# Two-layer trunk with an expert mixture: one product of two columns per item, smaller products in two levels, other order at entry and end

## The chip, the cores and the metric

One core of a Trainium2 chip runs the whole program. The metric is the device time of the program in microseconds, the median of repeated executions. The profile page and the trace come from one further execution.

## The reference

256 frames of width 1024 pass two layers, in fp32. Layer 0 is a gated mixer, a SwiGLU of width 2816 and a gated embedding; the change does not touch it. Layer 1 is a gated linear recurrence (HGRN2) with 8 heads of 128, the expert SwiGLU with 2 of 8 experts per frame, and again the gated embedding:

```python
def hgrn2(h, w_in, lb, o_norm_g, w_out):
    ...
    attn = jnp.einsum('bhtk,bhsk,bhtsk->bhts', qc, kc, decay)
    o = o_inter + jnp.einsum('bhts,bhsv->bhtv', attn, ic)
    ...
    o = rms_norm(o, o_norm_g.reshape(C_HEADS, C_HEAD_DIM)).reshape(bsz, s, C_WIDTH)
    return (o * jax.nn.silu(g)) @ w_out

def moe_swiglu(h, w_router, b_router, w_gu, w_down):
    logits = (h @ w_router) + b_router
    top_logit, top_idx = lax.top_k(logits, TOP_K)
    gates = ...
    for e in range(N_EXPERTS):
        out = out + gates[..., e:e + 1] * swiglu(h, w_gu[e], w_down[e])
    return out

gate = jax.nn.sigmoid(x @ ple_w_gate[layer])
x = x + gate * (p[layer] @ ple_w_proj[layer])
```

## The kernel before

**Products in three parts.** Every large weight is cut into granules of 128x2048 fp32, loaded by SP's DMAs. ScalarE rounds a granule to its high part (`hi`, L968, two instructions of 128x1024), VectorE subtracts to get the low part (`lo`, L1330, two instructions). A product is three matmuls of 512 columns, high by high, high by low and low by high (`split_matmul`, L451 to L453). The parts stand in a ring of 6 slots (`w_hi`, `w_lo`); the semaphores `hi_done`, `lo_done` and `used` keep the three engines in step.

**Items.** After the router, the frames of each expert are put in a list of up to 128, an item. Here 8 items run, 7 in the loop and the last behind it. An item has 7 units (`EU`) of 512 hidden columns: a unit's gate and up sides are four granules, 48 matmuls (`unit_gu`: side 0 and side 1), ScalarE takes the silu of side 0 (`unit_silu`, L1226), VectorE multiplies it by side 1 (`unit_hidden`, L1844), TensorE transposes the result (`unit_turn`, L863, 4 matmuls), ScalarE and VectorE evict it in two parts (`hT`: L1080, L1548), and the down product is two granules, 24 matmuls (`unit_down`). TensorE's order is: transposes of this unit, sides of the next one, down product of this unit, transposes of the next.

**What runs once per item.** VectorE selects the item's columns (`select`, L1784 and L1785) and compares them with a count (`compare`, L1789), which gives the one-hot matrix `sel` (frames by slots). TensorE gets from it, in the item's first unit, the frame that each slot is filled from (`turn_src`, L821, two matmuls of one column), and behind the last unit's transposes the row that each slot's result is written to (`turn_rows`: L835 adds a constant by the identity, L837 two matmuls of one column). VectorE turns both into integers (`origin`, L1868; `dst`). GpSimd gathers and stores rows by them. TensorE also transposes the gathered rows (`turn_xg`, L829).

**The entry.** The sides of the first unit are computed while the lists are made. ScalarE then waits for that product, then for the table's head (`table_ready`), and enters its loop. VectorE does `lo(77)`, `lo(78)`, select and compare, and then the first hidden product.

**The end.** Behind the last item VectorE evicts the transposed p (`pT(2)`, L1571), sums gates by rank and adds what was stored for each frame (`add_rows`, L1850 to L1858). TensorE does the last down product (`last_down`), puts the results back to frames by the transposed one-hot matrix (L944, L945; evictions L1285 and L1906), adds the projection of p (`proj_half`, 24 matmuls) and transposes the layer's output (`turn_x`, L502) for the gate.

**The recurrence's levels.** Within a block of 128 frames the decayed product of q and k is built in levels of doubling width. Before level n VectorE scales half of q and half of k (L1656, L1657); TensorE multiplies all heads (`level`, L702, 16 matmuls of 128x64); VectorE merges the result into the attention matrix under a mask (`meet`, L1634, 1.3 us). Between levels stand 12 matmuls of the input product. Behind them come the output's norm by head, a multiply of the silu gate by the norm's gain (`gains_of`, L1670) and the gate product (L1685).

## Time and profile before

| | |
|---|---|
| median of 3 executions | 1506.45 us (1506.19 to 1507.27) |
| profiled execution: its own time, its span | 1507.38 us, 1505.6 us |
| TensorE matmul busy | 98% of the span |
| TensorE weight load, VectorE, ScalarE busy | 81%, 83%, 66% |
| matmuls of the recurrence's levels 1 to 7 (L702) | 27.3 us |
| one item in the loop | 119.83 us |

### The profile page before, as it was taken

The page shows a single profiled execution, that of the slowest core. Times are in us where ns is not written, and L with a number is a line of the kernel's source. Part 1 is how long each engine was busy: PE and PEld are TensorE (multiplying, and loading weights), DVE is VectorE, ACT ScalarE, POOL GpSimd, SP SyncE. Part 2 cuts the span into 40 slices and gives each one's busy share as a digit, 9 for nine tenths or more (in the row PEclk, how much of TensorE's full clock was granted, in tenths as well). Part 3 has the DMA queues.
Part 4 walks back from the last instruction along what each step waited for, and adds up shares of the span by engine and source line. Part 5 has one row for each costly group of instructions (what it writes and reads, how often), then busy time and mean ns, then how long its engine had stood idle before and what let it go on. Part 6 is the DMA issues. An engine that isn't in the chain of part 4 may idle for free.

```text
span 1505.6 us, 23650 instructions
## 1 busy us (share of the span) xinstructions
PE 1474.3 (98%) x6913; PEld 1226.5 (81%) x6915; DVE 1244.1 (83%) x1544; ACT 1000.6 (66%) x1231; POOL 42.1 (3%) x43
## 2 busy tenths in 40 slices
PE   8999999999999899999999999999999999999988
PEld 6877888788887688888888888888888888888876
DVE  7996545574887989899988998899989889889985
ACT  6555444375225577787877877777787777778762
POOL 1000000000000200000000000000000000000000
PEclk9999999999999899999999999999999999999999
DMA  7666555555234899999999999999999999999960
GB/s 285 207 222 217 196 194 173 175 169 195 84 114 144 327 398 374 353 379 405 340 374 410 345 368 410 369 346 410 390 320 411 403 323 400 396 349 384 409 240 29
DMA packets 124743, 453.09 MB, mean 301 GB/s; under 512 B 13968, under 2 KB 13968, under 8 KB 124704
## 3 DMA queue, kind: packets, MB, share of 16 engines
q1 hardware_dynamic: 119952, 435.25, 77.3%
q0 software_dynamic: 4752, 17.34, 3.2%
q8 instruction: 22, 0.36, 0.1%
q14 instruction: 17, 0.14, 0.0%
HBM read 444.14 MB, written 8.39 MB: 301 GB/s over the span
## 4 chain that ended last, share of the span: by engine, by line
PE 92%; DVE 5%; ACT 1%; DMA 1%; issue 1%; SPq 0%; DVEq 0%; ACTq 0%
PE PS L451 29%; PE PS L453 28%; PE PS L452 28%; DVE w_lo L1330 2%; PE PS L863 2%; PE PS L702 2%; DMA raw<-in_w_in_ab 1%; PE PS L502 1%; PE PS L829 0%; ACT w_hi L968 0%; PE PS L588 0%; PE PS L809 0%; PE PS L697 0%; PE PS L746 0%; PE PS L685 0%
## 5 line engine op out<-in xcount | busy, mean ns | idle before, releaser
L1330 DVE TENSOR_TENSOR w_lo<-raw,w_hi 128x1024 fp32r<-128x1024 f32 x486 | 568.7, 1221 | 33.0 <-ACT w_hi L968 30.5
L451 PE MATMUL PS<-w_hi,xT_hi 128*128 128x512 f32 x1424 | 566.1, 398 | 5.1 <-DVE w_lo L1330 2.8
L453 PE MATMUL PS<-w_lo,xT_hi 128*128 128x512 f32 x1424 | 557.4, 391 | 0.0
L452 PE MATMUL PS<-w_hi,xT_lo 128*128 128x512 f32 x1424 | 556.3, 391 | 0.0
L968 ACT ACTIVATE w_hi<-raw 128x1024 fp32r<-128x1024 f32 x486 | 489.7, 1060 | 71.7 <-PE PS L453 44.6
L1330 DVE TENSOR_TENSOR w_lo<-SC,w_hi 128x1024 fp32r<-128x1024 f32 x340 | 392.0, 1220 | 10.9 <-ACT w_hi L968 9.3
L968 ACT ACTIVATE w_hi<-SC 128x1024 fp32r<-128x1024 f32 x340 | 337.5, 1060 | 15.3 <-PE PS L453 10.8
L451 PEld LDWEIGHTS PS<-w_hi,xT_hi 128*128 128x128 f32 x1424 | 269.8, 189 | 60.1 <-issue 5.3
L453 PEld LDWEIGHTS PS<-w_lo,xT_hi 128*128 128x128 f32 x1424 | 268.5, 189 | 57.6
L452 PEld LDWEIGHTS PS<-w_hi,xT_lo 128*128 128x128 f32 x1424 | 269.0, 189 | 53.5
L451 PE MATMUL PS<-w_hi,hT_hi 128*128 128x512 f32 x536 | 208.8, 390 | 4.2 <-DVE hT_lo L1548 4.2
L453 PE MATMUL PS<-w_lo,hT_hi 128*128 128x512 f32 x536 | 208.9, 390 | 0.0
L452 PE MATMUL PS<-w_hi,hT_lo 128*128 128x512 f32 x536 | 208.5, 389 | 0.0
L451 PEld LDWEIGHTS PS<-w_hi,hT_hi 128*128 128x128 f32 x536 | 100.6, 188 | 25.8 <-DVE hT_lo L1548 3.2
L453 PEld LDWEIGHTS PS<-w_lo,hT_hi 128*128 128x128 f32 x536 | 100.6, 188 | 20.9
L452 PEld LDWEIGHTS PS<-w_hi,hT_lo 128*128 128x128 f32 x536 | 100.6, 188 | 20.8
L1080 ACT ACTIVATE hT_hi<-PS 128x512 fp32r<-128x512 f32 x67 | 40.4, 603 | 98.0 <-PE PS L863 64.7
L1226 ACT ACTIVATE junk<-PS 128x512 f32<-128x512 f32 x56 | 33.5, 598 | 91.1 <-PE PS L453 91.0
L1548 DVE TENSOR_TENSOR hT_lo<-PS,hT_hi 128x512 fp32r<-128x512 f32 x67 | 46.3, 691 | 56.4 <-ACT hT_hi L1080 56.4
L1844 DVE TENSOR_TENSOR junk<-junk,PS 128x512 f32<-128x512 f32 x56 | 38.4, 686 | 32.5 <-ACT junk L1226 32.4
L863 PEld LDWEIGHTS PS<-ident,junk 128*128 128x128 f32 x224 | 35.4, 201 | 10.7 <-DVE junk L1844 6.5
L1542 DVE SCALAR_TENSOR_TENSOR junk<-PS,lbc,junk 128x256 f32<-128x256 f32 x22 | 9.6, 479 | 39.3 <-ACT junk L1074 39.3
(268 smaller groups left out, 640.5 us busy)
## 6 DMA issues: line engine op xcount, KB each, us to landing
raw<-in_e_w_gu SPq DMA_DIRECT2D x226, 512.0 KB, 7.5
SC<-in_e_w_gu SPq DMA_DIRECT2D x222, 512.0 KB, 7.1
SC<-in_e_w_down SPq DMA_DIRECT2D x114, 512.0 KB, 10.0
raw<-in_e_w_down SPq DMA_DIRECT2D x110, 512.0 KB, 6.9
raw<-in_ffn_w_gu SPq DMA_DIRECT2D x44, 512.0 KB, 4.5
raw<-in_w_in_c SPq DMA_DIRECT2D x32, 512.0 KB, 5.5
raw<-in_ffn_w_down SPq DMA_DIRECT2D x22, 512.0 KB, 3.9
raw<-in_w_in_ab SPq DMA_DIRECT2D x20, 512.0 KB, 7.7
```

The costliest lines, as they stand in the source:

```text
L451: pe.matmul(out, a_hi, b_hi, start=start, stop=False, skip_group_check=True)
L452: pe.matmul(out, a_lo, b_hi, start=False, stop=False, skip_group_check=True)
L453: return pe.matmul(out, a_hi, b_lo, start=False, stop=stop, skip_group_check=True)
L502: m = pe.transpose(PS[:, tile_bank(t, final) + b, j * P:(j + 1) * P], src[:, t, kt * P:(kt + 1) * P], ident[:, :])
L702: m = pe.matmul(PS[:, level_bank(n) + hd // 4, c:c + P // 2].rearrange("p (m w) -> p m w", w=w), kT[:, hd, tok], qT[:, hd, tok].rearrange( ...
L863: m = pe.transpose(PS[:, 2, c:c + P], hv[:, j, r, :], ident[:, :])
L968: act.activation(w_hi[:, g % RING, part], raw_part(g, s), ACT.Copy).then_inc(hi_done, 1)
L1080: act.activation(hT_hi[:, :], PS[:, b, :], ACT.Copy).then_inc(hT_act, 1)
L1226: act.activation(sg, PS[:, 0, :], ACT.Silu).then_inc(silu_done, 1)
L1330: dve.tensor_tensor(w_lo[:, g % RING, part], raw_part(g, s), w_hi[:, g % RING, part].bitcast(F32), ALU.subtract).then_inc(lo_done, 1)
L1548: dve.tensor_tensor(hT_lo[:, :], PS[:, b, :], hT_hi[:, :].bitcast(F32), ALU.subtract).then_inc(hT_ready, 1)
L1844: dve.tensor_tensor(hh, sg, PS[:, 1, :], ALU.mult).then_inc(h_ready, 1)
```

## The change

1. The two small products of an item become one of two columns, made in the item's first unit between side 0 and side 1. It is the next item's; the row number is kept by VectorE in `held`, with the constant added there. TensorE's wait on `dst_ready` goes; VectorE waits for the new product between `lo(8)` and `lo(9)`.
2. VectorE's first hidden product of an item moves ahead of the select, into the end of the previous item. At the entry it goes ahead of `lo(77)` and `lo(78)`, and ScalarE no longer waits for the sides' product ahead of the table.
3. Level 6 computes only the blocks that are used, 32 matmuls of 32x32 in place of 16 of 128x64, and level 7 16 of 64x64. VectorE's two merges for them go; ScalarE copies the blocks in three instructions.
4. The norm's gain multiplies the columns of the transposed evictions (`xT` with `V_ON`), four and four instructions of 128x128 per half in place of one and one of 128x512, and no longer the silu gate on VectorE. It is loaded by a small strided DMA; the list of gains is one shorter.
5. In the last item the rank sums stand before its loop, ScalarE scales the accumulator, the row additions stand before the last unit, `pT(2)` in it, and the first half of the projection ahead of the last down product.

The diff, cut to these:

```diff
-            def proj_half(layer, g, kk, turns=0):
+            def proj_half(layer, g, kk, turns=0, counts=(1, 1)):
...
-                m.then_inc(used, 1)
+                if counts[kk]:
+                    m.then_inc(used, counts[kk])
...
+                        elif n == 7:
+                            c = (hd % 4 * T + t) * (P // 2)
+                            half = slice(t * P, t * P + P // 2)
+                            m = pe.matmul(PS[0:P // 2, level_bank(7) + hd // 4, c:c + P // 2], kT[:, hd, half],
+                                          qT[:, hd, t * P + P // 2:(t + 1) * P], start=True, stop=True,
+                                          skip_group_check=True)
+                        elif n == 6:
+                            for m_ in range(2):
+                                a = m_ * (P // 2)
+                                c = (hd % 4 * T + t) * (P // 2) + m_ * 32
+                                m = pe.matmul(PS[a:a + 32, level_bank(6) + hd // 4, c:c + 32],
+                                              kT[:, hd, t * P + a:t * P + a + 32],
+                                              qT[:, hd, t * P + a + 32:t * P + a + 64], start=True, stop=True,
+                                              skip_group_check=True)
...
+            pe.wait_ge(attn_ready, 1)
...
-            def turn_src():
-
-                for t in range(T):
-                    m = pe.matmul(PS[:, 3, 1:2], sel[:, t, :], token[:, t:t + 1], start=(t == 0), stop=(t == T - 1),
-                                  skip_group_check=True)
-                m.then_inc(src_psum, 1)
-
...
             def turn_rows():
 
-                pe.matmul(PS[:, 3, 0:1], ident[:, :], marks[:, 3:4], start=True, stop=False, skip_group_check=True)
                 for t in range(T):
-                    m = pe.matmul(PS[:, 3, 0:1], sel[:, t, :], cur[:, 1, t:t + 1], start=False, stop=(t == T - 1),
+                    m = pe.matmul(PS[:, 3, 0:2], sel[:, t, :], pick[:, t, :], start=(t == 0), stop=(t == T - 1),
                                   skip_group_check=True)
                 m.then_inc(rows_psum, 1)
...
             def item(i, last):
                 unit_turn(i * EU + (FB + 1))
+                unit_gu(G_MOE + 4, i * EU, None, (0,))
                 if last:
                     turn_sel()
                 else:
                     pe.wait_ge(sel_ready, i + 2)
-                    turn_src()
-                unit_gu(G_MOE + 4, i * EU)
+                    turn_rows()
+                unit_gu(G_MOE + 4, i * EU, None, (1,))
                 pe.wait_ge(y_evac, i + 1)
                 unit_down(G_MOE + 8, i * EU + (FB + 1), False, i * EU, True)
                 unit_turn(i * EU + (FB + 2))
@@ -915,11 +933,11 @@
                     turn_xg(i + 1)
                 unit(EU - 2)
                 if last:
+                    pe.wait_ge(pT_ready, 2)
+                    proj_half(1, G_MOE, 0, i * EU + EU, (0, 2))
                     pe.wait_ge(selT_ready, 1)
                     last_down(G_MOE + ITEM - 2, i * EU + (FB + EU), i * EU)
                 else:
-                    pe.wait_ge(dst_ready, i + 2)
-                    turn_rows()
                     unit_gu(G_MOE + ITEM - 2, i * EU, i * 2 + 4)
                     unit_down(G_MOE + ITEM + 2, i * EU + (FB + EU), True, i * EU)
...
-            pe.wait_ge(pT_ready, 2)
-            for kk in range(2):
-                proj_half(1, G_MOE, kk, last_item * EU + EU)
+            proj_half(1, G_MOE, 1, last_item * EU + EU, (0, 2))
...
+            act.wait_ge(at_done, 7)
+            act.wait_ge(met, 1)
+            for a in range(0, P, P // 2):
+                c = a // 2
+                act.activation(attn[a:a + 32, :, :, a + 32:a + 64].rearrange("p h t n -> p (h t) n"),
+                               PS[a:a + 32, level_bank(6):level_bank(6) + 2, :].rearrange(
+                                   "p b (g n) -> p (b g) n", n=P // 2)[:, :, c:c + 32], ACT.Copy)
+            act.wait_ge(at_done, 8)
+            act.activation(attn[0:P // 2, :, :, P // 2:P].rearrange("p h t n -> p (h t) n"),
+                           PS[0:P // 2, level_bank(7):level_bank(7) + 2, :].rearrange("p b (g n) -> p (b g) n", n=P // 2),
+                           ACT.Copy).then_inc(attn_ready, 1)
...
+                    act.wait_ge(onorm_full, 16)
+                    xT(0, 4, V_ON)
             his(72, 74)
-            xT(1, 4, None)
+            xT(1, 4, V_ON)
```

```diff
+                    if last and end is None:
+                        pT(2)
...
                 if last:
-                    pT(2)
-                else:
+                    act.wait_ge(rank_ready, 1)
+                    act.wait_ge(y_loaded, 32)
+                    for t in range(T):
+                        act.activation(acc[:, t, :], acc[:, t, :], ACT.Copy, scale=by_rank[:, 0, t:t + 1]).then_inc(acc_scaled, 1)
+                unit(EU - 2, None if last else True)
...
             hi(G_MOE + 6)
-            product(G_MOE + 4)
             act.wait_ge(table_ready, 1)
```

```diff
                 dve.wait_ge(at_done, lv + 1)
-                if lv == 7:
-                    meet(7)
-                    dve.sem_inc(attn_ready, 1)
...
+                if lv < 6:
                     meet(lv)
+                if lv == 5:
+                    dve.sem_inc(met, 1)
...
             def gate_o(t):
-                step(gains_of((gg[:, t, N:D], gain[:, N:D]), 2 + t))
+                dve.wait_ge(g_evac, 2 + t)
                 dve.tensor_tensor(oo[:, t, :], oo[:, t, :], gg[:, t, :], ALU.mult).then_inc(o_ready, 1)
                 dve.wait_ge(o_ready, t + 1)
 
-            step(gains_of((gg[:, :, 0:N], gain[:, 0:N].unsqueeze(1).broadcast_to([P, T, N])), 1))
...
-                dve.tensor_copy(cur[:, 1, :].unsqueeze(2), row[:, :, bass.ds(col, 1)])
+                dve.tensor_copy(pick[:, :, 0:1], row[:, :, bass.ds(col, 1)])
...
-                dve.wait_ge(y_loaded, 32)
+                dve.sem_inc(rank_ready, 1)
+
+            def add_rows():
+
                 for t in range(T):
-                    step(dve.tensor_scalar(acc[:, t, :], acc[:, t, :], by_rank[:, 0, t:t + 1], None, ALU.mult))
+                    dve.wait_ge(acc_scaled, t + 1)
                     dve.scalar_tensor_tensor(out=acc[:, t, :], in0=xn[:, t, :], scalar=by_rank[:, 1, t:t + 1],
...
             def item(i, last):
-                unit_hidden(i * EU + (FB + 1))
                 lo(G_MOE + 7, i * EU)
                 hT(i * EU + (FB + 1), 2)
+                lo(G_MOE + 8, i * EU)
                 if not last:
-                    dve.wait_ge(src_psum, i + 1)
+                    dve.wait_ge(rows_psum, i + 2)
                     dve.tensor_copy(origin, PS[:, 3, 1:2]).then_inc(src_ready, 1)
-                lo(G_MOE + 8, i * EU)
                 lo(G_MOE + 9, i * EU)
 
                 def unit(u, end):
                     for q in (10, 11, 12):
                         lo(G_MOE + q, i * EU + u)
                     unit_hidden(i * EU + u + (FB + 2))
+                    if last and end is None:
+                        pT(2)
                     if end:
                         xg(i + 2)
-                        dve.wait_ge(rows_psum, i + 1)
+                        dve.wait_ge(rows_held, i + 1)
                         dve.wait_ge(rows_written, i * 16 + 16)
-                        dve.tensor_copy(dst, PS[:, 3, 0:1]).then_inc(dst_ready, 1)
+                        dve.tensor_copy(dst, held).then_inc(dst_ready, 1)
                     lo(G_MOE + 13, i * EU + u)
                     lo(G_MOE + 14, i * EU + u)
                     hT(i * EU + u + (FB + 2), 2)
                     lo(G_MOE + 15, i * EU + u)
 
+                if last:
+                    rank_gates()
                 with dve.Fori(0, EU - 2) as u:
                     unit(u, False)
-                unit(EU - 2, not last)
                 if last:
-                    pT(2)
                     add_rows()
-                else:
+                unit(EU - 2, None if last else True)
+                if not last:
                     for q in (4, 5, 6):
                         lo(G_MOE + ITEM + q, i * EU)
-
-            lo(G_MOE + 6)
+                    unit_hidden(i * EU + EU + (FB + 1))
+
+            dve.wait_ge(used, 2 * (G_MOE + 4))
+            unit_hidden(FB + 1)
+            los(G_MOE + 5, G_MOE + 7)
             with dve.Fori(0, last_item) as i:
                 dve.wait_ge(rows_psum, i + 1)
+                dve.tensor_scalar(held, PS[:, 3, 0:1], marks[:, 3:4], None, ALU.add).then_inc(rows_held, 1)
                 select(i + 2)
                 dve.wait_ge(cur_step, i + 2)
                 compare()
```

**TensorE, an item's first unit.** Before, the transposes are followed by the source tokens' product (`sel`, in `SC`, by the tokens, in `seg`) and then the sides; behind the last unit's transposes stand the row numbers (`marks` and `cur`):

```order
L863 MATMUL PS<-ident,junk 128x128 x4
...
L821 MATMUL PS<-seg,SC 128x1 x2
...
L451 MATMUL PS<-w_hi,xT_hi 128x512
L452 MATMUL PS<-w_hi,xT_lo 128x512
L453 MATMUL PS<-w_lo,xT_hi 128x512
```

```order
L863 MATMUL PS<-ident,junk 128x128 x4
L835 MATMUL PS<-marks,ident 128x1
L837 MATMUL PS<-cur,SC 128x1 x2
...
L451 MATMUL PS<-w_hi,xT_hi 128x512
L452 MATMUL PS<-w_hi,xT_lo 128x512
L453 MATMUL PS<-w_lo,xT_hi 128x512
```

After the change the sides' first 24 matmuls come at once, and the product of two columns behind them:

```order
L880 MATMUL PS<-ident,junk 128x128 x4
...
L460 MATMUL PS<-w_hi,xT_hi 128x512
L461 MATMUL PS<-w_hi,xT_lo 128x512
L462 MATMUL PS<-w_lo,xT_hi 128x512
...
L460 MATMUL PS<-w_hi,xT_hi 128x512
L461 MATMUL PS<-w_hi,xT_lo 128x512
L462 MATMUL PS<-w_lo,xT_hi 128x512
...
L854 MATMUL PS<-seg,SC 128x2 x2
...
L460 MATMUL PS<-w_hi,xT_hi 128x512
L461 MATMUL PS<-w_hi,xT_lo 128x512
L462 MATMUL PS<-w_lo,xT_hi 128x512
```

So behind either transposes the sides follow at once.

**VectorE, the entry of the loop.** Before, from the table's last cast to the lo part of the first transposes:

```order
L1837 CAST seg<-rt 1x5 [waits dve_step]
L1839 TENSOR_LOAD seg [waits table_ready]
...
L1330 TENSOR_TENSOR w_lo<-SC,w_hi 128x1024 [waits hi_done] x2
L1330 TENSOR_TENSOR w_lo<-raw,w_hi 128x1024 [waits hi_done] x2
...
L1784 COPY cur<-seg 128x2
...
L1785 COPY cur<-tab 128x2
L1789 TENSOR_SCALAR SC<-iota_c,cur 128x128 [waits cur_step]
...
L1844 TENSOR_TENSOR junk<-junk,PS 128x512 [waits silu_done]
...
L1548 TENSOR_TENSOR hT_lo<-PS,hT_hi 128x512 [waits hT_act]
```

After:

```order
L1863 CAST seg<-rt 1x5 [waits dve_step]
L1865 TENSOR_LOAD seg [waits table_ready]
...
L1869 TENSOR_TENSOR junk<-junk,PS 128x512 [waits silu_done,used]
L1362 TENSOR_TENSOR w_lo<-SC,w_hi 128x1024 [waits hi_done] x2
L1362 TENSOR_TENSOR w_lo<-raw,w_hi 128x1024 [waits hi_done] x2
...
L1932 TENSOR_SCALAR seg<-PS,marks_cur 128x1 [waits rows_psum]
...
L1810 COPY seg<-seg 128x2
...
L1811 COPY marks_cur<-tab 128x2
L1815 TENSOR_SCALAR SC<-iota_c,marks_cur 128x128 [waits cur_step]
...
L1580 TENSOR_TENSOR hT_lo<-PS,hT_hi 128x512 [waits hT_act]
...
L1362 TENSOR_TENSOR w_lo<-raw,w_hi 128x1024 [waits hi_done]
L1896 CAST seg<-PS 128x1 [waits rows_psum]
```

The hidden product (`junk` by `PS`) has moved ahead of two granules and the select, and waits for `used` too; the integer cast now waits for the product of two columns, one granule behind `hT_lo`.

**VectorE, the last unit.** Before, p and the row additions stand behind the last lo parts:

```order
L1548 TENSOR_TENSOR hT_lo<-PS,hT_hi 128x512 [waits hT_act]
...
L1330 TENSOR_TENSOR w_lo<-SC,w_hi 128x1024 [waits hi_done]
...
L1330 TENSOR_TENSOR w_lo<-SC,w_hi 128x1024 [waits hi_done]
L1571 TENSOR_TENSOR xT_lo<-SC,xT_hi 128x4x128 [waits pT_act]
...
L1850 ISA [waits dst_ready,rows_psum]
...
L1857 TENSOR_SCALAR SC<-SC,seg 128x1024 [waits y_loaded,dve_step]
L1858 SCALAR_TENSOR_TENSOR SC<-xn,seg,SC 128x1024 [waits dve_step]
L1857 TENSOR_SCALAR SC<-SC,seg 128x1024
L1858 SCALAR_TENSOR_TENSOR SC<-xn,seg,SC 128x1024 [waits dve_step]
L1906 TENSOR_TENSOR xT_lo<-PS,xT_hi 128x4x128 [waits ye_act,acc_done]
L1906 TENSOR_TENSOR xT_lo<-PS,xT_hi 128x4x128 [waits ye_act]
L1913 SCALAR_TENSOR_TENSOR SC<-PS,cur,SC 128x512 [waits scattered] x2
```

After, the additions stand ahead of the unit and p behind its hidden product:

```order
L1886 SCALAR_TENSOR_TENSOR SC<-xn,seg,SC 128x1024 [waits acc_scaled] x2
...
L1362 TENSOR_TENSOR w_lo<-SC,w_hi 128x1024 [waits hi_done]
...
L1362 TENSOR_TENSOR w_lo<-raw,w_hi 128x1024 [waits hi_done]
...
L1868 REGISTER_ALU
L1869 TENSOR_TENSOR junk<-junk,PS 128x512 [waits silu_done]
L1603 TENSOR_TENSOR xT_lo<-SC,xT_hi 128x4x128 [waits pT_act]
...
L1362 TENSOR_TENSOR w_lo<-raw,w_hi 128x1024 [waits hi_done]
...
L1580 TENSOR_TENSOR hT_lo<-PS,hT_hi 128x512 [waits hT_act]
...
L1362 TENSOR_TENSOR w_lo<-SC,w_hi 128x1024 [waits hi_done]
...
L1362 TENSOR_TENSOR w_lo<-SC,w_hi 128x1024 [waits hi_done]
L1940 TENSOR_TENSOR xT_lo<-PS,xT_hi 128x4x128 [waits ye_act] x2
```

So `hT_lo` has the additions and p ahead of it, and the down product's evictions (`xT_lo`, L1906, now L1940) no longer have them.

## Rows read from the trace of the kernel before

**Rows 1.** The page: busy time, and the chain that ended last, by engine.

```profile
PE 1474.3 (98%) x6913; PEld 1226.5 (81%) x6915; DVE 1244.1 (83%) x1544; ACT 1000.6 (66%) x1231; POOL 42.1 (3%) x43
...
PE 92%; DVE 5%; ACT 1%; DMA 1%; issue 1%; SPq 0%; DVEq 0%; ACTq 0%
```

**Rows 2.** TensorE's waits: us in total, times, longest.

```profile
PE PS L863 <- DVE junk L1844: 6.1, 1, 6.1
...
PE PS L702 <- DVEq L1659: 1.4, 1, 1.4
```

**Rows 3.** Timeline, weight loads at an item's boundary: start us, us, engine, instruction.

```profile
618.11 0.67 PEld L863 LDWEIGHTS PS<-ident,junk 128*128 128x128 f32 x4
...
635.60 0.67 PEld L863 LDWEIGHTS PS<-ident,junk 128*128 128x128 f32 x4
636.18 0.54 PEld L821 LDWEIGHTS PS<-seg,SC 128*128 128x128 f32 x4
...
652.89 0.67 PEld L863 LDWEIGHTS PS<-ident,junk 128*128 128x128 f32 x4
...
669.73 0.67 PEld L863 LDWEIGHTS PS<-ident,junk 128*128 128x128 f32 x4
```

**Rows 4.** Timeline, VectorE in an item's first and second unit.

```profile
637.58 0.69 DVE L1548 TENSOR_TENSOR hT_lo<-PS,hT_hi 128x512 fp32r<-128x512 f32 x1 [2.85 <-ACT hT_hi L1080]
...
649.89 0.68 DVE L1844 TENSOR_TENSOR junk<-junk,PS 128x512 f32<-128x512 f32 x1
```

**Rows 5.** Timeline, entry of the expert loop: VectorE, ScalarE, TensorE.

```profile
506.85 2.36 DVE L1330 TENSOR_TENSOR w_lo<-SC,w_hi 128x1024 fp32r<-128x1024 f32 x2 [0.96 <-DVE seg L1837]
...
512.07 0.68 DVE L1844 TENSOR_TENSOR junk<-junk,PS 128x512 f32<-128x512 f32 x1
...
528.67 0.69 DVE L1844 TENSOR_TENSOR junk<-junk,PS 128x512 f32<-128x512 f32 x1 [1.03 <-ACT junk L1226]
...
507.69 0.60 ACT L1226 ACTIVATE junk<-PS 128x512 f32<-128x512 f32 x1 [7.81 <-PE PS L453]
...
533.29 0.63 PE L863 MATMUL PS<-ident,junk 128*128 128x128 f32 x4
```

**Rows 6.** Stretches: us, busy of PE, PEld, DVE, ACT, POOL, then PEclk, DMA.

```profile
408.00:412.00 4.00, 4.00 (x15) 3.61 (x16) 2.90 (x3) 1.17 (x2) 0.00 (x0) 0.50 0.65 208
...
512.00:518.00 6.00, 5.20 (x17) 4.43 (x18) 6.00 (x9) 4.04 (x5) 1.36 (x1) 0.50 0.91 298
...
1468.00:1470.00 2.00, 2.00 (x8) 1.55 (x7) 2.00 (x4) 1.53 (x5) 0.00 (x0) 0.63 0.05 8
1470.00:1472.00 2.00, 2.00 (x7) 1.54 (x6) 1.75 (x10) 1.74 (x2) 0.00 (x0) 0.52 0.00 0
```

**Rows 7.** Timeline, levels 6 and 7 and the gate: TensorE, then VectorE.

```profile
420.88 3.68 PE L702 MATMUL PS<-SC 128*128 128x64 f32 x32
...
427.22 3.68 PE L702 MATMUL PS<-SC 128*128 128x64 f32 x32
...
424.60 1.22 DVE L1656 TENSOR_TENSOR SC<-SC 128x1024 f32<-128x1024 f32 x1
425.74 1.22 DVE L1657 TENSOR_TENSOR SC<-SC 128x1024 f32<-128x1024 f32 x1
...
447.10 0.69 DVE L1670 TENSOR_TENSOR xn<-xn,gain 128x512 f32<-128x512 f32 x1 [1.23 <-ACT xn L1181]
```

**Rows 8.** Timeline, end of the last item: VectorE, then TensorE.

```profile
1457.35 0.69 DVE L1548 TENSOR_TENSOR hT_lo<-PS,hT_hi 128x512 fp32r<-128x512 f32 x1 [0.33 <-ACT hT_hi L1080]
...
1464.85 1.28 DVE L1858 SCALAR_TENSOR_TENSOR SC<-xn,seg,SC 128x1024 f32<-128x1024 f32 x1
...
1458.28 0.49 PE L451 MATMUL PS<-w_hi,hT_hi 128*128 128x512 f32 x1 [1.59 <-DVE hT_lo L1548]
...
1466.91 0.50 PE L944 MATMUL PS<-xT_hi,selT 128*128 128x512 f32 x1 [2.92 <-DVE xT_lo L1906]
...
1478.15 0.49 PE L451 MATMUL PS<-w_hi,xT_hi 128*128 128x512 f32 x1 [1.05 <-DVE xT_lo L1403]
```

50 lines of the change are left out of this document (26 added, 24 removed).

## The prediction

> **What bounds the kernel now.** I read the page first: TensorE is busy 98% of the span and carries 92% of the chain that ended last [rows 1]. So time goes only where TensorE gets fewer instructions or waits less. The second view is what TensorE waits for [rows 2]: one wait of 6.1 us for the hidden product of the first expert unit, one of 1.4 in the recurrence's levels, and at the end of the last item 1.6, 2.9 and 1.1 us [rows 8]. The third is the timeline around an item's boundary [rows 3, 4], the fourth the entry of the expert loop [rows 5], and then the granted clock [rows 6], since an idle stretch can be paid twice. Last come levels 6 and 7 [rows 7] and the end of the last item [rows 8].
>
> The profiled execution took 1507.38 us for a span of 1505.6; the median is 1506.45, 0.9 us lower. The sum is made against the profiled one and carried to the median as it is. About 0.2%, 3 us, can be told from no change.
>
> **Row numbers and source tokens.** From one hidden transpose to the next, the weight loads take 669.73 - 652.89 = 16.84 us in a plain unit. The unit that has the row numbers behind its transposes takes 635.60 - 618.11 = 17.49, and the one with the source tokens 652.89 - 635.60 = 17.29 [rows 3]. So three products cost 0.65 and two cost 0.45, 0.22 each though they move one column: 0.54 us of weight loading is four passes of 0.13. Two columns should cost what one does. The new product has two matmuls, 0.45, but stands inside a stream of large matmuls, between side 0 and side 1. An own stop in the stream costs little: 72 large matmuls of 0.2267 are 16.32 us, the four transposes make it 16.84, so 0.52 where four single passes of 0.11 would be 0.44. I add 0.07 (bounds 0 and 0.2). Per item 0.65 + 0.45 - 0.45 - 0.07 = 0.58, times 7 items: **-4.1 us** (bounds -3.2 and -4.6). The wait on the row numbers' copy goes too, but nothing in the trace waits there.
>
> The change adds a wait: VectorE now stops between the lo parts 8 and 9 until the new product is done. The item's transposes start at 635.6, 0.52 us; side 0 is 24 matmuls, 5.4 us; the product is done near 642.1. VectorE has the hidden transposes' lo part at 637.58 and is through one granule more (two L1330, 2.3 us) at 640.5 [rows 4]. So it stands 1.7 us. Behind it are four granules and then the hidden product of the next unit, now at 649.89 + 0.69 = 650.6. TensorE wants it at 652.9 [rows 3], a slack of 2.3. It is left with 0.6. So it costs nothing; with the cover gone, each further 0.1 us is paid seven times. The gather of the next frames starts some 4 us later, with five units left to hide it.
>
> **Entry of the loop.** Now VectorE takes lo(77), lo(78), selects and compares, and reaches the hidden product at 512.07 [rows 5]; TensorE idles 6.1 us [rows 2], from about 506.5. After the change the hidden product comes first. ScalarE's silu no longer stands in front of the table but behind it; it began at 507.69 before [rows 5] and I expect it at 507, so the hidden product at 507.5 to 507.9. TensorE's idle shrinks to about 1.7. But VectorE's work up to the hidden product of the second unit is the same: 528.67 - 506.85 is 21.8 us of which 1.2 is idle, so 20.6, and from 507.9 this gives 528.5 and an end at 529.2. TensorE started those transposes at 533.29, so it starts them at 529.6 at the latest: **-3.7 us** (bounds -3.4 and -4.1) and not the 4.4 of the first idle. In between, TensorE at full clock has done its 72 matmuls by 525.7 and waits 3.5 us. The idle of 2.9 us at the end of the kernel was followed by a granted clock of 0.63 and 0.52 for two stretches of 2 us [rows 6], 0.74 + 0.96 = 1.7 us of full-speed work. I charge this here, +1.7 (bounds 0 and the 3.4 us of twice that length): **-2.0 us** net. The 6.1 us idle had cost half clock for the whole of 512 to 518 [rows 6], but VectorE, not TensorE, set the end of that unit, so nothing is won there beyond the 3.7.
>
> **Levels 6 and 7.** A level is 16 matmuls, 32 passes in 3.68 us, 0.115 each [rows 7], the same as with one column [rows 3]; no row has less than 128 weight columns. For level 7, 16 matmuls of 64 by 64, the bounds are 3.7 us (price by pass) and 1.8 (price by weight columns). Level 6 has 32 matmuls of 32 by 32: 7.4 by pass, 1.8 by columns. But level 6 can win nothing: level 7's product waits for VectorE's q and k, which run at 424.60 and 425.74 and end at 426.9, with TensorE at 427.22. VectorE is held there by lo parts until 424.60, and the merge that goes stood behind q and k. So level 6 gives 0 (bounds 0 and +3.7) and level 7 between 0 and -1.9. I take -1.5: one-column products already show that what streams through sets no price, which leaves the weights. The gain multiply of 0.69 us before the gate product [rows 7] lies on the path, since TensorE's next transposes follow it with little room: -0.2. The wider evictions that take its place, eight small ones for two, cost ScalarE and VectorE some 0.5 us each per half, and large matmuls cover them. The removed merges, 1.3 us each on VectorE, are covered too. The gain's load, 1024 values on GpSimd's queue, is done long before its use. **-1.7 us** (bounds +3.7 and -2.1).
>
> The Trainium skill, TensorE: Matmul & The Clock Gate, section LDWEIGHTS, says that a weight load takes its number of columns over 1.2, in ns, whatever the rows; by this, called an estimate, level 7 comes to 1.7 us. The trace's 0.11 us for 128 columns agrees. Against it stands the Trainium skill, TensorEngine Tiling (Array Packing), Key Properties: a change of tiling mode drains the engine. No run here shows one.
>
> **The end.** The last item's rank sums move ahead of its loop, the scaling to ScalarE, the two row additions of 1.28 us [rows 8] and the last transposes of p ahead of or into the last unit. TensorE has 12 projection matmuls, 2.7 us, in place of its wait of 1.6 before the last down product [rows 8]. VectorE is then the late one: 2.6 us of additions and 0.6 of p stand ahead of the hidden lo part, which was at 1457.35 [rows 8] with 1.4 us of idle in that unit, so it ends near 1459.9 and the down product starts at 1460.0 instead of 1458.3. The down product's first half is then evicted 1.7 us later than before, but without the additions behind it the scatter starts at 1465.8 in place of 1466.9. From there 8 scatter matmuls and 12, not 24, projection matmuls: done at 1471.2. VectorE's chain from scatter to the layer output took 5.6 us; its transposes start at 1472.3, and the part that started at 1478.15 [rows 8] at 1475.05: **-3.1 us** at full clock (bounds -2 and -4). TensorE idles 1.1 and 1.7 us there, between the 1.6 us that left the clock whole and the 2.9 that did not; I charge +1.7 once more, so **-1.4**.
>
> Sum: -4.1 - 2.0 - 1.7 - 1.4 = -9.2, so **1497.3 us** (the profiled execution 1498.2).
>
> **Rivals.**
> - The clock stays whole in both places: -12.6, 1493.9 us. For it: 1.6 us of idle at 1458 was followed by full clock. Against: 3.5 us at the entry is longer than the 2.9 that brought it down. Chance 0.25.
> - The small products cost by pass or by the change of tile: level 6 doubles to 7.4 us and level 7 wins nothing. +3.7 - 0.2 in place of -1.7: 1502.5 us. It also fails by the clock: at 408 to 412 it stood at 0.50 [rows 6] after the wait of 1.4 us in a level [rows 2]; some 3.5 us at half speed more would give 1500.8. Against: weights are a quarter as wide. Chance 0.22. The rule of the Trainium skill on a change of tiling mode (TensorEngine Tiling (Array Packing), Key Properties) would act in this rival.
> - VectorE's new wait makes the hidden product late in each item. It decides from a delay of 2.3 us on, and I expect 1.7. If ScalarE, semaphores and the copy make it 3 us, TensorE idles 0.7 us seven times: +4.9, 1502 us; if each idle also halves the clock for a stretch (1.7 us), +16.8, 1514 us, slower than before. For it: slack is 0.6 us by the rows. Against: the clock was whole after the waits of 1.1 and 1.6 us [rows 8]. Chance 0.09, 0.05 of it slower.
> - The change does nothing where VectorE binds, at entry and end: then -4.1 and -1.7, 1500.6 us. Chance 0.07.
> - As forecast: 0.37.
>
> **Numbers.** Slower by over 3 us: 0.05, the third rival. Within 3 us: the second rival with a failing end, 0.07. Faster: 0.88. The range reaches from a little below the whole clock (1492.8) to above the doubled level (1502.8).
>
> **What will show it.** The hidden transposes of a unit in the loop: 16.84 us for five units and 17.36 for the first, the period 119.83 down to 119.25. TensorE's wait for the hidden product: 6.1 us replaced by about 1.7 and 3.5, the second unit's transposes at 529 to 530 less what the levels gave. Level 6 and level 7 as groups of 64 and 32 passes, with level 7 still starting some 2.3 us behind VectorE's q. At the end, no wait of 2.9 us at the scatter. The clock rows by 2 us around both places decide the first rival. Wrong would be: TensorE idle before each item's second unit, level 6 over 4 us, or a loop period that hasn't fallen.

## The result, and the profile after

The changed kernel takes 1498.89 us (median of 6 executions, 1493.77 to 1502.67), the kernel before, in turn with it, 1506.92. The medians differ by 8.0 us. The ratio is 0.9944, with a 95% interval of 0.9930 to 0.9958: 8.4 us faster, 6.3 to 10.5. Forecast were 9.2 us and 1497.3. The profiled execution took 1497.92 us for a span of 1496.2. The kernel before keeps within 2 us, the changed one spreads over 9.

The page, busy time and chain by engine, for [rows 1]:

```profile
PE 1465.4 (98%) x6903; PEld 1215.8 (81%) x6903; DVE 1237.6 (83%) x1556; ACT 1004.9 (67%) x1248; POOL 45.9 (3%) x43
...
PE 89%; DVE 7%; issue 1%; ACT 1%; DMA 1%; SPq 0%; ACTq 0%; DVEq 0%
```

TensorE is still the bound; VectorE's share of the chain has risen from 5 to 7%. TensorE's waits, for [rows 2] (us in total, times, longest):

```profile
PE PS L880 <- DVE junk L1869: 4.3, 2, 2.6
PE PS L460 <- DVE w_lo L1362: 3.4, 3, 1.6
PE PS L460 <- DVE hT_lo L1580: 3.2, 3, 1.4
...
PE PS L712 <- DVEq L1688: 2.6, 1, 2.6
...
PE PS L821 <- DVEq L1784: 1.5, 1, 1.5
PE PS L726 <- DVEq L1688: 1.4, 1, 1.4
```

The wait of 6.1 us has become two, of 1.6 and 2.6, and there is a new one of 2.6 ahead of level 7 (L712). The weight loads at an item's boundary, for [rows 3]:

```profile
614.26 0.67 PEld L880 LDWEIGHTS PS<-ident,junk 128*128 128x128 f32 x4
...
631.10 0.67 PEld L880 LDWEIGHTS PS<-ident,junk 128*128 128x128 f32 x4
...
637.06 0.64 PEld L854 LDWEIGHTS PS<-seg,SC 128*128 128x128 f32 x4
...
648.45 0.67 PEld L880 LDWEIGHTS PS<-ident,junk 128*128 128x128 f32 x4
...
665.29 0.67 PEld L880 LDWEIGHTS PS<-ident,junk 128*128 128x128 f32 x4
```

The unit behind the first row takes 16.84 us where it took 17.49, and the next one, with the product of two columns (L854) in it, 17.35 where it took 17.29. VectorE in the same item, for [rows 4]:

```profile
633.08 0.69 DVE L1580 TENSOR_TENSOR hT_lo<-PS,hT_hi 128x512 fp32r<-128x512 f32 x1 [2.07 <-ACT hT_hi L1096]
...
637.83 0.16 DVE L1896 CAST seg<-PS 128x1 int32<-128x1 f32 x1 [1.44 <-PE PS L854]
...
647.01 0.69 DVE L1869 TENSOR_TENSOR junk<-junk,PS 128x512 f32<-128x512 f32 x1
```

The integer cast waits 1.44 us for the product (forecast 1.7). The hidden product ends at 647.7, TensorE's load is at 648.45, so 0.75 us of the slack are left (forecast 0.6). The entry, for [rows 5], VectorE, then TensorE:

```profile
506.78 0.69 DVE L1869 TENSOR_TENSOR junk<-junk,PS 128x512 f32<-128x512 f32 x1 [1.70 <-ACT junk L1254]
...
527.01 0.68 DVE L1869 TENSOR_TENSOR junk<-junk,PS 128x512 f32<-128x512 f32 x1
...
507.52 0.74 PE L880 MATMUL PS<-ident,junk 128*128 128x128 f32 x4 [1.61 <-DVE junk L1869]
...
527.75 0.74 PE L880 MATMUL PS<-ident,junk 128*128 128x128 f32 x4 [2.64 <-DVE junk L1869]
```

The granted clock, for [rows 6] (the number behind POOL's count is PEclk):

```profile
426.00:428.00 2.00, 2.00 (x16) 1.79 (x15) 1.94 (x3) 0.60 (x1) 0.00 (x0) 0.50 0.37 104
428.00:430.00 2.00, 2.00 (x8) 1.60 (x7) 1.76 (x2) 0.42 (x1) 0.00 (x0) 0.65 0.81 242
...
488.00:490.00 2.00, 2.00 (x6) 0.85 (x5) 1.97 (x4) 0.71 (x2) 0.00 (x0) 0.50 0.93 320
...
528.00:530.00 2.00, 2.00 (x9) 1.62 (x9) 2.00 (x3) 1.47 (x3) 1.72 (x1) 0.60 1.03 422
530.00:532.00 2.00, 2.00 (x7) 1.57 (x6) 2.00 (x2) 1.87 (x3) 2.00 (x1) 0.55 1.04 412
...
1468.00:1470.00 2.00, 2.00 (x6) 1.52 (x6) 1.83 (x9) 1.01 (x1) 0.00 (x0) 0.50 0.00 0
```

There are four stretches of some 4 us at half clock, at 426, 487, 528 and 1467, beside the span's last 2 us. By the same view over their whole length each takes 1.7 us of full-speed work. The kernel before had one at 406 to 414, twice as long, one at the entry, three times as long, and one at the end. Levels 5 to 7, for [rows 7], with the first row of the weighing of values (L770), and then VectorE:

```profile
411.46 3.79 PE L726 MATMUL PS<-SC 128*128 128x64 f32 x32
...
417.97 1.21 PE L719 MATMUL PS<-SC 128*32 128x32 f32 x64
...
424.72 2.64 PE L712 MATMUL PS<-SC 128*64 128x64 f32 x32 [2.60 <-DVEq L1688]
...
431.13 1.95 PE L770 MATMUL PS<-SC 128*128 128x128 f32 x16
...
419.98 2.36 DVE L1362 TENSOR_TENSOR w_lo<-raw,w_hi 128x1024 fp32r<-128x1024 f32 x2 [0.52 <-DVE SC L1666]
```

Level 6 takes 1.21 us for 64 passes. Level 7 follows after a wait, and its own 2.64 us lie partly at half clock. The end, for [rows 8], VectorE, then TensorE:

```profile
1450.95 0.69 DVE L1580 TENSOR_TENSOR hT_lo<-PS,hT_hi 128x512 fp32r<-128x512 f32 x1
...
1452.04 0.49 PE L460 MATMUL PS<-w_hi,hT_hi 128*128 128x512 f32 x1 [0.57 <-DVE hT_lo L1580]
...
1459.19 0.50 PE L962 MATMUL PS<-xT_hi,selT 128*128 128x512 f32 x1 [0.62 <-DVE xT_lo L1940]
...
1467.13 0.79 PE L460 MATMUL PS<-w_hi,xT_hi 128*128 128x512 f32 x1 [1.34 <-DVE xT_lo L1435]
```

Counted from the weight load of the last unit's transposes (1447.8, before 1455.83), the last down product starts after 4.2 us, the scatter's second part after 11.4 and the last row after 19.3; before, the last row came after 22.3.

**Where the 9.4 us of span went.** Between the same instructions of both profiles: up to level 5, -3.1; level 5 to the output's transposes (before 414.54 to 449.10, after 411.46 to 446.47), +0.45; from there to the third unit's transposes, -1.2; to the last unit's, -4.1; to the end, -1.5. The first stands where no instruction was changed: level 4 took 5.23 us before, at half clock, and 3.79 after, with the same wait ahead of it, and what follows up to level 5 was at half clock too.

### The profile page after: what moved, and what is told of

It is laid out like the page before. It is cut to its first block, busy times and chain, and to the rows that moved or that the text cites. A ratio compares the mean times of both kernels' runs of the same rounds, so it can differ in the third digit from the quotient of the medians.

```text
span 1496.2 us, 23664 instructions
## 1 busy us (share of the span) xinstructions
PE 1465.4 (98%) x6903; PEld 1215.8 (81%) x6903; DVE 1237.6 (83%) x1556; ACT 1004.9 (67%) x1248; POOL 45.9 (3%) x43
## 4 chain that ended last, share of the span: by engine, by line
PE 89%; DVE 7%; issue 1%; ACT 1%; DMA 1%; SPq 0%; ACTq 0%; DVEq 0%
PE PS L460 28%; PE PS L462 28%; PE PS L461 28%; DVE w_lo L1362 3%; PE PS L880 2%; DMA raw<-in_w_in_ab 1%; PE PS L511 0%; PE PS L726 0%; DVE SC L1666 0%; PE PS L847 0%; ACT w_hi L984 0%; DVE SC L1685 0%; DVE SC L1686 0%; PE PS L597 0%; PE PS L834 0%
## 5 line engine op out<-in xcount | busy, mean ns | idle before, releaser
L1254 ACT ACTIVATE junk<-PS 128x512 f32<-128x512 f32 x56 | 33.5, 598 | 88.8 <-PE PS L462 88.8
```

The costliest lines, as they stand in the source:

```text
L1254: act.activation(sg, PS[:, 0, :], ACT.Silu).then_inc(silu_done, 1)
```

## The experiments

Most experiments set two theories against each other. By theory A, each part of the change is worth what its own place says, and the clock adds or takes 1.7 us where TensorE idles. By the rivals (B, C), places or sizes matter otherwise: a small product costs by its place, small levels save, VectorE's stop is paid, idle time is free. What A and B say in one case stands in the expectation. All ratios are to the kernel before. Each kernel but the tenth is the changed one with the edit shown. Where a profile is compared, the distance between two instructions is taken, since the load of the first weights shifts whole profiles by 1 us or so.

**1. Level 6 wide again.**

```diff
-                        elif n == 6:
-                            for m_ in range(2):
...
```

> The changed kernel, but level 6 is again 16 matmuls of 128x64. Theory A (level 6 gives nothing, and its shrinking only opens an idle stretch of 2.6 us before level 7 that brings half clock): level 6 takes 3.7 us, the wait before level 7 falls to about 0.2 us, no clock below 1.00 at 426 to 430, the start of the transposes behind the gate product (446.5) comes 1 to 2 us earlier, and the run is the same or up to 2 us faster. Rival B (the small level is a real saving): TensorE loses the 2.5 us that the level grows by, +2.5 us.

Measured: 1497.53 us (1495.04 to 1501.14), ratio 0.9942 (0.9923 to 0.9962). The timeline of TensorE, levels 6 and 7 and what follows:

```profile
418.86 3.78 PE L718 MATMUL PS<-SC 128*128 128x64 f32 x32
...
425.68 2.08 PE L712 MATMUL PS<-SC 128*64 128x64 f32 x32 [0.23 <-DVEq L1680]
...
430.55 1.95 PE L762 MATMUL PS<-SC 128*128 128x128 f32 x16
```

The wait is 0.23 us, level 7 takes 2.08 us, and the clock is 1.00. Level 6 is 2.6 us longer, and from level 6 to level 7 it is 6.82 us instead of 6.75: the small level saves nothing. Level 5 to the output's transposes takes 33.5 us, 1.5 less than in the changed kernel. Theory A holds in the profile; the medians (1.4 us) differ by less than their spread.

**2. The product of two columns ahead of side 0.**

```diff
-                unit_gu(G_MOE + 4, i * EU, None, (0,))
...
-                unit_gu(G_MOE + 4, i * EU, None, (1,))
+                unit_gu(G_MOE + 4, i * EU)
```

> The changed kernel, but the product of two columns stands right behind the item's transposes, ahead of side 0. Theory A (the gain of the items is the number of small products, not their place): the item's first unit takes 17.3 us as now (17.35), the period stays 119.24, VectorE no longer stands before the integer cast, the time is the same to 1 us. Rival B (the place matters, since a stop in the stream of large matmuls costs its own start): 0.1 to 0.2 us less or more per item, 1 us in all. Rival C (TensorE now waits for the compare): an idle stretch before the product in each item, at least 0.3 us times 7.

Measured: 1501.30 us (1497.73 to 1501.80), 0.9954 (0.9937 to 0.9970). In the loop the unit takes 17.29 us instead of 17.35: the own stop costs 0.06, forecast 0.07, and no idle stands there. But the median is 2.4 us above the changed kernel's, where I expected the same to 1 us. What I had not expected is the first item, where the compare is behind two granules of lo parts:

```profile
514.70 1.02 PE L854 MATMUL PS<-seg,SC 128*128 128x2 f32 x4 [4.59 <-DVE SC L1814]
```

TensorE waits 4.6 us there and the second unit's transposes come 25.1 us behind the first (20.2 in the changed kernel), with half clock in between. So the place matters, at the entry, through VectorE's order: rival C, in the first item alone.

**3. The product 12 matmuls later.**

```diff
                 unit_gu(G_MOE + 4, i * EU, None, (0,))
+                unit_gu(G_MOE + 4, i * EU, None, (1,), (0,))
...
-                unit_gu(G_MOE + 4, i * EU, None, (1,))
+                unit_gu(G_MOE + 4, i * EU, None, (1,), (1,))
```

> The changed kernel, but the product of two columns is 12 matmuls (2.7 us) later, in the middle of side 1; VectorE's stop before the integer cast grows from about 1.7 to 4.4 us. The theory of the slack (2.3 us until TensorE is kept waiting): the hidden product of the item's second unit is 2 us late, TensorE waits about 2 us once per item, seven times: +14 us, and up to 1.7 us more for each item in which the clock falls to one half behind it, so +14 to +26 us. Rival (VectorE catches up, or the wait is hidden by the silu's lateness): less than +3 us.

Measured: 1509.43 us (1507.31 to 1511.17), 1.0013 (1.0004 to 1.0023), 10.5 us above the changed kernel by the medians, below the 14 to 26 us that I expected. VectorE and TensorE in an item of the loop:

```profile
642.48 0.16 DVE L1897 CAST seg<-PS 128x1 int32<-128x1 f32 x1 [4.16 <-PE PS L854]
...
651.67 0.68 DVE L1870 TENSOR_TENSOR junk<-junk,PS 128x512 f32<-128x512 f32 x1
...
652.41 0.74 PE L880 MATMUL PS<-ident,junk 128*128 128x128 f32 x4 [1.64 <-DVE junk L1870]
```

The stop is 4.16 us, and TensorE waits 1.64 us. The unit takes 19.36 us and the next 16.73, 1.9 us more than in the changed kernel. That is paid in six items and not in seven: in the loop's first item TensorE waits 2.6 us for the hidden product with either kernel. The last item adds 1.0 us, so from the third unit's transposes to the last unit's it is 914.2 us instead of 901.8, 12.4 more. The clock behind that wait:

```profile
652.00:654.00 2.00, 1.59 (x9) 1.42 (x10) 2.00 (x3) 0.81 (x2) 0.00 (x0) 1.00 1.03 422
654.00:656.00 2.00, 2.00 (x11) 1.63 (x10) 2.00 (x3) 2.00 (x3) 0.00 (x0) 1.00 1.03 422
```

It stays at 1.00, in all six items. The slack is near what the rows said: 2.7 us more of stop cost 1.9, so some 0.8 was left. The prediction's third rival had the mechanism and the price per item right, but not its half clock.

**4. The first hidden product behind two granules.**

```diff
-            unit_hidden(FB + 1)
             los(G_MOE + 5, G_MOE + 7)
+            unit_hidden(FB + 1)
```

> The changed kernel, but at the entry of the loop the first hidden product is again behind lo(77) and lo(78). Theory A (VectorE's total work sets the second unit's transposes, so moving the hidden product gains only what TensorE's 72 matmuls were late): first transposes 4 us later, second ones 1 to 2 us later at full clock, 3 to 4 if the idle stretch of about 6 us brings half clock, but then no idle of 2.6 us before the second: +1 to +3 us. Rival B (the whole first idle is on the path): +4.5 us or more.

Measured: 1499.49 us (1498.26 to 1500.63), 0.9950 (0.9934 to 0.9967). TensorE waits 5.5 us for the first transposes, at half clock behind it, and not at all for the second. From the gate's transposes to the third unit's it is 98.9 us, against 97.9 in experiment 1, which has no half clock before the table. Both figures hold the half clock at their own wait. So the early hidden product is worth 1.0 us net and not the 4 of the first idle stretch: theory A, at its lower edge. The medians (0.6 us) can't tell this.

**5. The projection behind the scatter.**

```diff
-                    pe.wait_ge(pT_ready, 2)
-                    proj_half(1, G_MOE, 0, i * EU + EU, (0, 2))
...
-            proj_half(1, G_MOE, 1, last_item * EU + EU, (0, 2))
+            pe.wait_ge(pT_ready, 2)
+            for kk in range(2):
+                proj_half(1, G_MOE, kk, last_item * EU + EU)
```

> The changed kernel, but both halves of the last projection are behind the scatter again (VectorE as changed). Theory A (the projection half fills a wait of TensorE and leaves the path behind the scatter): TensorE waits about 3 us ahead of the last down product, the down product starts at the same time, the output's transposes start where 12 more matmuls end, some 1.6 us later (2.7 less the 1.1 that TensorE waited there), and a half clock stretch of 1.7 us stands in the projection instead of behind it: +1.6 us, +1 to +3.5 with the clock. Rival B (the layer output's chain on VectorE covers the 12 matmuls): 0.

Measured: 1499.70 us (1498.81 to 1500.52), 0.9949 (0.9933 to 0.9966). TensorE at the last down product and at the last row of [rows 8]:

```profile
1453.46 0.49 PE L460 MATMUL PS<-w_hi,hT_hi 128*128 128x512 f32 x1 [3.17 <-DVE hT_lo L1580]
...
1471.30 0.49 PE L460 MATMUL PS<-w_hi,xT_hi 128*128 128x512 f32 x1 [1.05 <-DVE xT_lo L1435]
```

From the last transposes to the last row it takes 21.6 us against 19.1, with half clock at 1454 to 1458 before the row, where the changed kernel has it behind. To the end of the span it is 1.0 us more: the lower edge of theory A.

**6. The row additions behind the last unit.**

```diff
-                if last:
-                    add_rows()
                 unit(EU - 2, None if last else True)
-                if not last:
+                if last:
+                    add_rows()
+                else:
```

> The changed kernel, but VectorE's two row additions stand behind the last unit again (the scaling stays on ScalarE). Theory A (they only change places between two points of the path): the last down product starts 2.5 us sooner, directly behind the projection half, but the additions of 2.5 us then stand beside it, done before its first half is evicted: 1 to 2.5 us faster than the changed kernel, since they now fit into VectorE's wait. Rival B (they delay the evictions as in the kernel before, by 2 us): 0 to +1 us.

Measured: 1496.54 us (1494.36 to 1500.52), 0.9933 (0.9913 to 0.9953). TensorE at the scatter and at the last row:

```profile
1459.89 0.50 PE L962 MATMUL PS<-xT_hi,selT 128*128 128x512 f32 x1 [0.56 <-DVE xT_lo L1940]
...
1467.82 0.49 PE L460 MATMUL PS<-w_hi,xT_hi 128*128 128x512 f32 x1 [1.34 <-DVE xT_lo L1435]
```

That is 10.25 and 18.18 us behind the last transposes (1449.64), 0.9 us less than in the changed kernel (11.12 and 19.06). No half clock stands ahead of these rows in the last part of either profile. So moving the additions ahead of the last unit, a part of the change, cost 0.9 us. The 1 to 2.5 us of theory A were a little too much.

**7. The hidden product ahead of lo(12).**

```diff
-                    for q in (10, 11, 12):
-                        lo(G_MOE + q, i * EU + u)
+                    lo(G_MOE + 10, i * EU + u)
+                    lo(G_MOE + 11, i * EU + u)
                     unit_hidden(i * EU + u + (FB + 2))
+                    lo(G_MOE + 12, i * EU + u)
```

> The changed kernel, but in every unit of the loop VectorE takes the hidden product ahead of lo(12), two instructions of 2.3 us in all. Theory A (at the entry VectorE sets the second unit's transposes, and the idle of 2.6 us there brings half clock): the second unit's transposes come 2.3 us earlier, the idle falls to 0.3 us, there is no half clock at 528 to 532, all other units keep 16.84 us: -2.3 us at the second unit and -1.5 us more at the third, -3.8 us in all. Rival B (the lo part is late in its place, or VectorE waits for the silu): units longer than 16.84 us, no gain.

Measured: 1495.66 us (1494.19 to 1498.91), 0.9931 (0.9914 to 0.9947). The second unit's transposes:

```profile
526.39 0.74 PE L880 MATMUL PS<-ident,junk 128*128 128x128 f32 x4 [0.36 <-DVE junk L1869]
```

They come 17.94 us behind the first ones (20.22 in the changed kernel), and the third unit's 16.73 behind these (18.31): -3.9 us. The clock:

```profile
528.00:530.00 2.00, 2.00 (x11) 1.62 (x10) 2.00 (x3) 2.00 (x3) 2.00 (x1) 1.00 1.02 408
```

It is whole. All later units keep their times. VectorE's order set the second unit, as forecast, and with the idle stretch the half clock went. What I had not expected is the last unit: its `hT_lo` comes later, TensorE waits 1.7 us ahead of the last down product (0.6 in the changed kernel), and from the load of the last transposes to the end it is 47.9 us without half clock up to the last microseconds, where the profiles of experiments 2, 3, 4 and 11, also without it, have 46.6 to 46.8. So this edit gives 3.9 us at the entry and takes 1.1 at the end.

**8. Zeros into the wait ahead of level 7.**

```diff
+            pe.wait_ge(met, 1)
+            for _ in range(10):
+                pe.matmul(PS[:, level_bank(7), :], zeros[:, 0:P], zeros[:, :], start=True, stop=True,
+                          skip_group_check=True)
             level(7)
```

> The changed kernel, but TensorE fills the idle stretch ahead of level 7 with 10 matmuls of zeros by zeros, 2.2 us (work that counts for nothing). Theory A (the idle stretch brings the half clock at 426 to 430): clock 1.00 there, level 7 in 2.1 us, the product behind it 1.5 us sooner, the time 1 to 1.6 us lower, or the same if the clock falls at another place instead. Rival B (the small matmuls of the levels themselves bring it): half clock at 426 to 430 all the same, 0 or +0.3 us.

Measured: 1497.46 us (1494.34 to 1499.62), 0.9938 (0.9920 to 0.9957). Level 7 and what follows:

```profile
425.82 2.08 PE L712 MATMUL PS<-SC 128*64 128x64 f32 x32 [0.41 <-DVEq L1692]
...
430.71 1.95 PE L774 MATMUL PS<-SC 128*128 128x128 f32 x16
```

4.89 us between them, where the changed kernel takes 6.41; the clock is 1.00. The work is the same but for useless matmuls in idle time, so the idle stretch is the cause of the half clock: 1.5 us. This doesn't rest on one execution: the 7 profiles with a wait of 2.4 to 2.6 us ahead of level 7 all have half clock behind it, and the 7 without the wait (both of the kernel before, experiments 1, 8, 9, 11 and 12) have none.

**9. Edits 1, 6 and 7 together.**

> The changed kernel with three edits at once: level 6 wide again, the hidden product ahead of lo(12) in each unit, the row additions behind the last unit. If the places are independent, as the theory of separate waits says: 3.9 us off at the second and third unit, 0.9 at the end, and no half clock ahead of level 7 (1.5) nor in the last part (up to 1.7): 1491 to 1495 us. Rival (a saved idle stretch only moves the half clock to another place): 1494 to 1498 us.

Measured: 1494.41 us (1491.19 to 1496.68), 0.9920 (0.9903 to 0.9936). The profiled execution, 1491.19, has one stretch of half clock, at 1460 to 1464, in the last part. At the entry and in the levels the parts add up: level 5 to the output's transposes takes 33.5 us, as in experiment 1, and the first three units take the times of experiment 7. At the end they don't: from the load of the last transposes to the end it is 48.5 us, 0.2 more than in the changed kernel (48.3), each with one stretch of half clock. The 0.9 us of experiment 6 don't show, since edit 7 takes as much there. The median lies in the range of either theory and doesn't decide between them.

**10. The kernel before once more.**

> The kernel before, unchanged, for a second profile of it. Theory A (the half clock at 406 to 414 belongs to this kernel, since its times spread over 2 us only, and a missing stretch of 3 us would show): half clock at 406 to 414 again, the levels as before, the same time. Rival B (that stretch comes and goes as in the changed kernel, and something else gives the time back): no half clock there, and another stretch of the same price in its place.

Measured: 1507.57 us (1503.68 to 1508.28), 1.0002 (0.9992 to 1.0011); the profiled execution is the one of 1503.68. Levels 4 and 5:

```profile
405.67 3.79 PE L702 MATMUL PS<-SC 128*128 128x64 f32 x32 [1.39 <-DVEq L1659]
...
412.22 3.79 PE L702 MATMUL PS<-SC 128*128 128x64 f32 x32
```

Level 4 has its wait of 1.39 us and takes 3.79 us, at full clock, and no other stretch stands in its place. So theory A falls, since the stretch can be missing in this kernel too, and rival B with it, since nothing gives the time back: the execution is 3.7 us below the one profiled first. Of that, 3.1 us lie between level 4 and level 5 and 1.4 at the entry, where the half clock is a third shorter; the profile's start takes 0.8 back. By the times that is rare (22 of the 23 executions of this kernel here took more than 1505 us), while only 3 of the 11 profiles of changed kernels with this wait (the changed one, experiments 1 to 9 and 11) show the stretch. Why it is nearly always there in the kernel before stays open.

**11. Both levels undone.**

```diff
-                        elif n == 7:
-                        elif n == 6:
...
-                if lv < 6:
+                if lv < 7:
                     meet(lv)
```

> The changed kernel with levels 6 and 7 undone: 16 matmuls of 128x64 for both, VectorE merges both, ScalarE copies nothing. Theory A (level 7's smaller product is worth 1.5 us of TensorE at full clock, level 6's nothing, and the added wait ahead of level 7 took it back in half clock): level 5 to the first weighing of values 19.0 us as in the kernel before (19.7 in the changed one, 18.1 with only level 6 undone), clock 1.00 there, the time within 1.5 us of the changed kernel. Rival B (the smaller levels are a gain of 3 us or more by themselves): 1502 us or more.

Measured: 1497.42 us (1493.84 to 1499.15), 0.9935 (0.9915 to 0.9954). Level 7 and what follows:

```profile
424.52 3.68 PE L712 MATMUL PS<-SC 128*128 128x64 f32 x32
...
430.86 1.95 PE L756 MATMUL PS<-SC 128*128 128x128 f32 x16
```

Level 5 (411.65) to the weighing of values takes 19.2 us, and to the output's transposes 34.6, against 35.0 in the changed kernel and 33.5 with level 6 alone undone. So part 3 of the change costs 0.4 us as it is made, and gives 1.1 us if level 6 stays wide.

**12. The three edits, and two idle stretches filled.**

```diff
+            pe.wait_ge(met, 1)
+            for _ in range(6):
+                pe.matmul(PS[:, level_bank(4), :], zeros[:, 0:P], zeros[:, :], start=True, stop=True,
+                          skip_group_check=True)
             level(4)
...
             unit_gu(G_MOE, 0, 2)
+            warm(6)
```

> The kernel with the three edits, and TensorE fills two idle stretches with matmuls of zeros: 6 ahead of level 4 (1.3 of the 1.4 us of waiting at 405) and 6 ahead of the loop's first transposes (1.3 of 1.6 us). Theory A (any of these stretches can bring half clock in a run): clock 0.998 or more, spread between runs smaller, 1489 to 1492 us. Rival B (half clock comes from the small matmuls and transposes as much as from idle time): no difference from the kernel with the three edits.

Measured: 1492.67 us (1491.66 to 1493.25), 0.9901 (0.9885 to 0.9918), the fastest here and 6.2 us below the changed kernel. It is 1.7 us below experiment 9, but the intervals overlap, so by the times rival B is not excluded. The waits for the hidden products:

```profile
PE PS L876 <- DVE junk L1866: 0.6, 2, 0.3
```

and level 4:

```profile
405.45 3.79 PE L718 MATMUL PS<-SC 128*128 128x64 f32 x32 [0.22 <-DVEq L1685]
```

The spread is 1.6 us over 4 executions, where the changed kernel has 9 over 6 and experiment 9 has 5.5 over 4. Two stretches of half clock are left in the profile, ahead of the table (486 to 490) and at 1462 to 1466, so theory A's clock of 0.998 was a little too high, and its range too low by 0.7 us.

## Why the prediction was right, and where not

- **Items: right.** Forecast -4.1 us; from the third unit's transposes to the last unit's it is 901.8 us against 905.9. Two columns cost what one does (17.29 us for the unit in experiment 2 and before), the product's own stop 0.06 us, and VectorE's stop of 1.44 us is covered, with 0.75 us left. No experiment brings the second product back; the gain is read from these distances.
- **Entry: right in its mechanism, with one idle stretch smaller.** I forecast waits of 1.7 and 3.5 us and a net gain of 2.0. They are 1.6 and 2.6. My 3.5 left out that the new product of two columns, some 0.5 us, stands in this unit of TensorE. The distance from the gate's transposes to the third unit's is 97.9 us without other half clock (experiments 1 and 8), 99.4 and 100.8 in the two profiles of the kernel before: -1.5 and -2.9. In the pair profiled first it is only -1.2, since the changed kernel has a stretch of half clock at 487, ahead of the table, which I had not counted. The stretch charged for the second idle came in each of the 7 profiles that have a wait of 2.6 us there and in none of the 3 that removed it.
- **Levels: wrong.** The step that failed is "level 6 gives 0", with a cost only if the small products were slow. Level 7 gave about what I took, -1.6 for -1.5 (3.68 to 2.08 us). The gate's multiply gave 0.2. But the removed time of level 6 became a wait of 2.6 us, and half clock behind it took 1.5 us back; I had charged just this at two other places, and here only within the second rival (3.5 us). And VectorE lost 0.5 us at its new increment of `met`, which stands between a merge and the next lo part: the row at 419.98 shows 0.52 us of waiting for the merge, where the kernel before and experiment 11, both without this increment, have none. In sum +0.45 instead of -1.7. The rival's price, level 6 by pass, was far off: 1.2 us and not 7.4. A change of tile costs little here: the rows name tiles of 128*32 and 128*64, and level 6 starts 0.32 us behind the last large matmul where the wide one of experiment 1 starts 0.23 behind it.
- **End: right, with the clock a matter of chance.** The scatter's first part starts 10.0 us behind the last transposes, as forecast (1465.8 on the old scale). The last row of [rows 8] comes 3.0 us sooner (forecast 3.1), and the span's end 1.5 us sooner (forecast 1.4), since half clock follows the row, where the kernel before has it ahead of it. That stretch stands in 5 of the 11 profiles with this end or that of experiment 6. In experiment 11 it doesn't, and the end is 46.6 us behind the last transposes instead of 48.3. The row additions ahead of the last unit cost 0.9 us of this gain.
- **The sum: near, and partly by luck.** The forecast was 9.2 us and 8.4 were measured. But the four parts come to 6.4 us in the profiles (1.2, 4.1 and 1.5 less 0.45), 2.8 short: the levels by 2.1 and the entry by 0.8. What made up for it there is the 3.1 us ahead of level 5, where the kernel before had half clock and the changed one had not, and which no term of the forecast held. Over the executions the clock gives less: the mean granted clock listed with each is 0.9947 over the six of the changed kernel and 0.9938 over the 13 of the kernel before beside experiments 1 to 4, by my estimate 1.2 us of a span of 1500. Whether the change made the stretch ahead of level 5 rarer stays open. The range was right in its size, for the reason given: the clock.

## What to carry to other kernels

Work that TensorE is spared ahead of a wait isn't saved: it becomes idle time, and the clock can take a second price for it. So look at what releases the next instruction before a product is made smaller, and where the idle stretch can't be removed, reorder the other engine's queue for it (experiment 7) or fill it. Where VectorE sets the pace for one unit only, a wanted product can pass granules that have room in every later unit; but look at the last unit too, where it cost 1.1 us here.

## What the hardware showed that I had not expected

- **Half clock by idle time.** Waits of TensorE of 2.4 to 2.6 us were followed by half clock in 14 of 14 places (level 7 in 7 profiles, the second unit in 7), each costing 1.5 to 1.7 us. Waits of 1.4 us ahead of level 4 were followed by it in 4 of 13 profiles, waits of 1.3 to 1.5 us ahead of the table in 6 of 14, and waits of 1.64 us inside the large matmuls in none of 6, all in one profile. So the same wait has different effects in different executions. That these waits make the spread between executions is not shown: it is 9 us in the changed kernel and 1.6 in experiment 12, where most are gone, but also 1.7 in experiment 5, which has them all.
- **Small products are cheaper than their share.** A pass took 0.115 us with 128 weight columns, 0.065 with 64 and 0.019 with 32 (3.68 us for 32 passes, 2.08 for 32, 1.21 for 64). From 128 to 32 columns this is a sixth, not a quarter. The rule of the Trainium skill, TensorE: Matmul & The Clock Gate, section LDWEIGHTS, columns over 1.2 in ns, gives 0.107, 0.053 and 0.027: the measured value is above it at 128 and 64 and below it at 32, and the measurement decides. From 64 to 32 the moving columns were halved too, so the last step is not the weights' alone. In level 6 neighbouring matmuls write different partitions of PSUM; whether they overlap for that reason was not tried.
